# A fused two-block layer on one core: the second block's input norm and the gate bias moved to VectorE, prefix sums and clears to GpSimd, the residual's norm to the output projection, the first head pair reordered

## The reference

```python
def chunked_spatial_gating(xc, ln_g, ln_b, w_s, b_s):
    z = jax.nn.gelu(xc)
    u, v = jnp.split(z, 2, axis=-1)
    v = layernorm(v, ln_g, ln_b).reshape(B, L // CHUNK, CHUNK, N_GMLP_HEADS, GMLP_HEAD_DIM)
    g = jnp.einsum('bnpec,eqp->bnqec', v, w_s) + b_s.T[:, :, None]
    return u * g.reshape(B, L, D_GMLP)

    x = x + (jax.nn.silu(gate) * val) @ ffn_w_down[i]      # end of the first block
    return rmsnorm(x, norm_final)

def hybrid_layer(x, mem, ...):                             # the second block
    h = rms_norm(x, norm_g)
    proj = h @ w_in
    (aq, ak, av, az, br, bk, bv, bz, bwd, bad, cq, cz, ga, gb, gc) = jnp.split(proj, offsets, axis=-1)
    aq = rms_norm(aq, a_q_g); ak = rms_norm(ak, a_k_g)
    ya = chunked_band_attention(aq, ak, av, a_rel_bias) * jax.nn.silu(az)
    yb = rwkv7_time_mix(br, bk, bv, bwd, bad, ...) * jax.nn.silu(bz)
    yc = memory_cross_attention(cq, mk, mv) * jax.nn.silu(cz)
    merged = sigmoid(ga) * (ya @ w_up_a) + sigmoid(gb) * (yb @ w_up_b) + sigmoid(gc) * (yc @ w_up_c)
    return x + merged @ w_o
```

## Time and profile before

| | us |
|---|---|
| median of 3 runs (2471.11 to 2479.15) | 2474.42 |
| profiled execution | 2478.68 |
| its span, first to last instruction | 2477.0 |
| PE busy | 2413.2 |
| DVE busy | 1535.6 |
| ACT busy | 1134.2 |
| GpSimd busy | 12.8 |

### The profile page before, as it was taken

One profiled execution on the slowest core, in us unless ns is written; L12 is line 12 of the kernel. 1 busy time (PEld: TensorE's weight loads), 2 busy tenths in 40 slices (PEclk: granted clock), 3 DMA queues, 4 the chain that ended last, 5 costly groups with the idle time before them and its releaser, 6 DMA issues.

```text
span 2477.0 us, 50747 instructions
## 1 busy us (share of the span) xinstructions
PE 2413.2 (97%) x19960; PEld 2374.3 (96%) x19960; DVE 1535.6 (62%) x2064; ACT 1134.2 (46%) x1463; POOL 12.8 (1%) x27
## 2 busy tenths in 40 slices
PE   6999999999999999996999999999999999999999
PEld 6899999999999999996899999999998999999999
DVE  6556576666546666567866676766566455555554
ACT  5343345555434555434444455444465444444443
POOL 0000000000000000000000000000000000000000
PEclk9999899999999999998999999999999999999999
DMA  6453355555555555554333333332355455555554
GB/s 236 141 187 116 125 185 184 184 185 186 187 187 187 186 186 186 186 185 132 120 125 100 115 116 114 121 127 98 118 188 168 139 171 189 189 189 182 196 187 161
DMA packets 110142, 400.32 MB, mean 162 GB/s; under 512 B 12394, under 2 KB 12421, under 8 KB 109904
## 3 DMA queue, kind: packets, MB, share of 16 engines
q1 hardware_dynamic: 108000, 391.00, 47.3%
q0 software_dynamic: 2032, 7.67, 1.0%
HBM read 396.52 MB, written 2.10 MB: 161 GB/s over the span
## 4 chain that ended last, share of the span: by engine, by line
PE 92%; DVE 5%; issue 1%; ACT 1%; DMA 0%; DVEq 0%; SPq 0%; ACTq 0%
PE bank L418 91%; DVE scratch L1393 1%; DVE w_lo L1344 1%; ACT w_hi L917 1%; PE bank L620 1%; DVE h_lo L1390 0%; DVE s_k L1393 0%; DMA x<-in_xT 0%; DVE cum L1390 0%; DVE ping L1390 0%; DVE s_t L1390 0%; DVE root L1432 0%; DVE qr L1871 0%; DVE acc L1390 0%; DVE s_t L1397 0%
## 5 line engine op out<-in xcount | busy, mean ns | idle before, releaser
L1344 DVE TENSOR_TENSOR w_lo<-raw,w_hi 128x1024 fp32r<-128x1024 f32 x736 | 896.4, 1224 | 787.9 <-ACT w_hi L917 783.1
L917 ACT ACTIVATE w_hi<-raw 128x1024 fp32r<-128x1024 f32 x736 | 778.6, 1060 | 1086.0 <-PE bank L418 1062.3
L418 PE MATMUL bank<-h_hi,w_hi 128*128 128x256 f32 x4016 | 1149.8, 286 | 19.8 <-issue 8.3
L418 PE MATMUL bank<-h_lo,w_hi 128*128 128x256 f32 x4016 | 1125.9, 280 | 0.0
L418 PE MATMUL bank<-h_hi,w_lo 128*128 128x256 f32 x4016 | 1122.0, 279 | 0.0
L418 PEld LDWEIGHTS bank<-h_hi,w_hi 128*128 128x128 f32 x4016 | 758.7, 189 | 28.8 <-issue 14.2
L418 PEld LDWEIGHTS bank<-h_lo,w_hi 128*128 128x128 f32 x4016 | 759.1, 189 | 3.3 <-issue 2.2
L418 PEld LDWEIGHTS bank<-h_hi,w_lo 128*128 128x128 f32 x4016 | 758.3, 189 | 0.0
L418 PE MATMUL bank<-m_hi,w_hi 128*128 128x256 f32 x704 | 197.8, 281 | 0.0
L418 PE MATMUL bank<-m_lo,w_hi 128*128 128x256 f32 x704 | 197.1, 280 | 0.0
L418 PE MATMUL bank<-m_hi,w_lo 128*128 128x256 f32 x704 | 195.7, 278 | 0.0
(11 more groups left out here) (413 smaller groups left out, 2773.1 us busy)
## 6 DMA issues: line engine op xcount, KB each, us to landing
raw<-in_units SPq DMA_DIRECT2D x736, 512.0 KB, 3.3
x<-in_xT SPq DMA_DIRECT2D x4, 512.0 KB, 5.9
memx<-in_memT POOLq DMA_DIRECT2D x4, 512.0 KB, 7.4
out_y<-obuf SPq DMA_DIRECT2D x8, 256.0 KB, 4.2
bias_t<-in_bias POOLq DMA_DIRECT2D x8, 192.0 KB, 2.8
dft<-in_dft POOLq DMA_DIRECT2D x1, 1024.0 KB, 7.7
decay<-in_decay POOLq DMA_DIRECT2D x1, 768.0 KB, 5.8
con<-in_con SPq DMA_DIRECT2D x1, 546.0 KB, 8.1
```

The source lines that it names most:

```text
L418: return pe.matmul(out, lhsT, rhs, start=start, stop=stop, skip_group_check=True)
L917: return act.activation(out, in_, ACT.Copy, scale=scale)
L1344: dve.tensor_tensor(w_lo[slot][:, :, :], raw[slot][:, :, :], w_hi[slot][:, :, :].bitcast(F32), ALU.subtract).then_inc(split_done, 1)
```

## The change

1. The gate bias `bs` is loaded to all partitions, and DVE adds it when it reads the bank; the one-row matmuls go.
2. During the last down projection `x` times the two gains (without any norm) is split into `h_hi`/`h_lo`, quarter by quarter. `root3` is applied instead by DVE wherever a product of the second block leaves PSUM: `lx`, pr, pk, pv, k0, qk, avf, az, `cqs`, `czs`, and each merge gate. ACT no longer reads these banks; it applies Square, Tanh or Silu to what DVE wrote. `root3` moves to memory of its own, and the row root of the first block to `row_root`, over parameters no longer used.
3. The narrow projection's units 0 to 2 come first, then unit 0 of the first pair, then narrow unit 3 (SP's order of loading follows). The norm's sums on PE come after the first pair's unit 1, the rate matmuls at k = 3 to 5, three at a time.
4. Prefix sums are on GpSimd, the first pair's alone first; six clears and the ones of `ep` too. GpSimd's loads of the bias for heads 1 to 7 stand behind them in its queue.
5. In each pair the sum of the squared queries on PE goes from k = 12 to 13, its root on ACT to k = 13 behind the exponentials, the reciprocal on DVE from `late` to k = 14.
6. `x` is scaled by the first block's norm in the output projection, a pair of tiles ahead of each addition.

```diff
@@ gpsimd
+            pool.dma_start(bs[:, :, :].rearrange("p e q -> p (e q)"), a["bs"].broadcast_to([P, HY * P]))\
...
+            for t in ("a", "b", "k", "v", "Nt", "Kt"):
+                pool.memset(bd[t][:, :, :], 0.0).then_inc(zeroed, 1)
...
+            pool.wait_ge(rates_ready, 1)
+            for pairs, other in ((slice(0, 1), ping[0]), (slice(1, 8), ping[1])):
+                here, there = (t.rearrange("p g (c t) -> p (g c) t", t=CHUNK)
+                               for t in (cum[:, pairs, :], other[:, :, :]))
+                for b in range(6):
+                    src, dst = ((here, there), (there, here))[b % 2]
+                    s = 1 << b
+                    pool.tensor_tensor(dst[:, :, s:CHUNK], src[:, :, s:CHUNK], src[:, :, 0:CHUNK - s], ALU.add)\
+                        .then_inc(prefix_step, 1)
+                    pool.tensor_copy(dst[:, :, 0:s], src[:, :, 0:s]).then_inc(prefix_step, 1)
+                    steps += 2
+                    pool.wait_ge(prefix_step, steps)
+                pool.memset(spare[:, 2:3], 0.0).then_inc(prefix_done, 1)
@@ tensor
-                    mm(o, gvt[:, c, e * P:(e + 1) * P], ws[:, e, :], True, False)
-                    m = mm(o, con[0:1, CC["ones"][0]:CC["ones"][0] + P], bs[0:1, e * P:(e + 1) * P], False, True)
+                    m = mm(o, gvt[:, c, e * P:(e + 1) * P], ws[:, e, :])
...
-            norm_sums(acc_x, acc_g)
-            group(1, h_hi, h_lo, tiles=1, arriving=True)
+            def lora_unit(u):
+                pe.wait_ge(dve_for_pe, tiles_in[2 * u + 1])
+                unit(2, UK * u, h_hi, h_lo, u == 0, u == 3, 1)
+            for u in range(3):
+                lora_unit(u)
...
-                if k == 12:
+                if k == 13:
                     pe.wait_ge(sums_read, n.next("sums"))
                     pe.wait_ge(qk_squared, n.next("qk"))
...
-                from_act()
+                pe.wait_ge(bank_read[1], n.now(("fill", 1)))
                 for c in range(2):
                     m = pe.transpose(banks[7][:, c * P:(c + 1) * P], avf[:, c * P:(c + 1) * P], ident)
...
             for k in range(16):
                 heads(k)
+                if k == 0:
+                    lora_unit(3)
                 if k == 1:
+                    norm_sums(acc_x, acc_g)
+                if k == 3:
                     from_act()
                     pe.wait_ge(lora_in, 16)
@@ scalar, heads(k, g)
                 if k == 11:
-                    act.activation(qr[:, :, :], p2(0), ACT.Square).then_inc(qk_squared, 1)
-                    copy(qk[:, :, :], p2(0)).then_inc(bank_read[0], 1)
-                if k == 12:
-                    act.wait_ge(qk_sums, n.next("qk"))
-                    to_dve(act.activation(flat(qr), banks[7][:, :], ACT.Sqrt, bias=con_("eps6"), scale=1.0 / P))
+                    act.wait_ge(bank_read[0], n.now(("fill", 0)))
+                    act.activation(qr[:, :, :], qk[:, :, :], ACT.Square).then_inc(qk_squared, 1)
                 if k == 13:
+                    if isinstance(g, int):
+                        act.wait_ge(zeroed, 7)
+                    act.wait_ge(prefix_done, 1 if isinstance(g, int) else 2)
...
                     to_dve(m)
+                    act.wait_ge(qk_sums, n.next("qk"))
+                    to_dve(act.activation(flat(qr), banks[7][:, :], ACT.Sqrt, bias=con_("eps6"), scale=1.0 / P))
                 if k == 15:
-                    to_pe(copy(avf[:, :], p2(1)[:, 0, :]))
-                    to_dve(act.activation(az[:, :], p2(1)[:, 1, :], ACT.Tanh, scale=0.5))
+                    from_dve()
+                    to_dve(act.activation(small["en"][:, :], az[:, :], ACT.Tanh, scale=0.5))
@@ vector
+                    if half:
+                        for s, b in enumerate(pair):
+                            own_bank(b)
+                            gained_pair(4 * q + 2 * s, lambda t: gains[:, 1, bass.ds(t, 1)])
+                        for s in range(2):
+                            low_pair(4 * q + 2 * s)
+                        for s in range(2 if q < 3 else 0):
                             running(4 * q + 2 * s, q == 0 and s == 0, gained=True)
...
+            split4()
+            running(12, False, gained=True)
+            running(14, False, gained=True)
             to_pe(dve.memset(lx[:, 0:1], 0.0))
...
-            normalised(x, lambda t: gains[:, 1, t:t + 1], scratch2, h_hi, h_lo, root3)
-            step(dve.reciprocal(root2[:, :], root2[:, :]))
@@ vector, heads(k, g)
+                if k == 3:
+                    step(tt(sm["pr"][:, 1:T + 1], p2(0)[:, 0, :], root3[:, :], ALU.mult))
+                    read(tt(sm["pk"][:, 1:T + 1], p2(0)[:, 1, :], root3[:, :], ALU.mult), 0)
+                if k == 7:
+                    to_act(tt(sm["k0"][:, :], p2(1)[:, 1, :], root3[:, :], ALU.mult))
+                    read(tt(sm["pv"][:, 1:T + 1], p2(1)[:, 0, :], root3[:, :], ALU.mult), 1)
+                if k == 11:
+                    read(tt(qk[:, :, :], p2(0), bcast(root3[:, :], 2), ALU.mult), 0)
+                if k == 15:
+                    to_act(tt(az[:, :], p2(1)[:, 1, :], root3[:, :], ALU.mult))
+                    read(tt(avf[:, :], p2(1)[:, 0, :], root3[:, :], ALU.mult), 1)
...
+                if k == 14:
+                    from_act()
+                    step(dve.reciprocal(flat(qr), flat(qr)))
@@ vector, late(units, g)
-                read(stt(az[:, :], az[:, :], 1.0, p2(1)[:, 1, :], ALU.add, ALU.mult), 1)
-
-                step(dve.reciprocal(flat(qr), flat(qr)))
+                step(stt(az[:, :], sm["en"][:, :], 1.0, az[:, :], ALU.add, ALU.mult))
@@ vector, merge and output
+                        group_done()
+                        read(tt(gate[:, :, :], p2(0), bcast(root3[:, :], 2), ALU.mult), 0)
                         split4(2)
-                        own_bank(0)
+                        from_act()
...
+            step(dve.reciprocal(row_root, row_root))
+            settle()
+            def normed_pair(tile):
+                for s in range(2):
+                    t = x[:, bass.ds(tile + s, 1), :].rearrange("p o t -> p (o t)")
+                    step(stt(t, t, col("norm_final", tile + s), row_root, ALU.mult, ALU.mult))
+                settle()
```

More of the change, by code:

```diff
@@ L603, in _ @@
                         m.then_inc(unit_used, 1)
-            norm_sums(acc_x, acc_g)
-            group(1, h_hi, h_lo, tiles=1, arriving=True)
+            tiles_in = [n.next("dve") for _ in range(8)]
+            pe.wait_ge(bank_read[2], n.now(("fill", 2)))
+            n.next(("fill", 2))
+            def lora_unit(u):
[3 more added lines that the diff above has]
+                lora_unit(u)
             ident = con_("ident")
@@ L1272, in _ @@
                     high_halves(scratch3, mh_hi, quarters=MEM_SPLIT[h])
[L1273 removed]
                 n.next(("fill", h % 2))
[L1275 removed]
+                act.wait_ge(bank_read[h % 2], n.now(("fill", h % 2)))
+                cz = czs[:, 2 * h:2 * h + 2, :]
+                act.activation(cz, cz, ACT.Silu).then_inc(cross_gates, 1)
             def key_root():
@@ L1629, in _, with residual @@
             gated(2, last=True)
-            def residual(tile, b, out=None):
+            def residual(tile, b):
                 group_done()
@@ L1634, in residual @@
                 t = x[:, bass.ds(tile, 2), :]
-                dst = t if out is None else out[:, bass.ds(tile, 2), :]
-                read(tt(dst, t, p2(b), ALU.add), b)
+                read(tt(t, t, p2(b), ALU.add), b)
             step(dve.memset(acc_x[:, :, :], 0.0))
@@ L1839, in queries @@
                 if k % 4 == 3:
-                    n.next(("fill", (k // 4) % 2))
+                    h, b = k // 4, (k // 4) % 2
+                    n.next(("fill", b))
+                    group_done()
+                    read(tt(cqs[:, 2 * h:2 * h + 2, :], p2(b), bcast(root3[:, :], 2), ALU.mult), b)
             def y_tile(i):
@@ L2050, in _ @@
             settle_pe()
-            with n.loop(4, {"unit": 36, "act": 2, "to_act": 2, "step": 2, ("fill", 0): 6, ("fill", 1): 6,
+            with n.loop(4, {"unit": 36, "act": 8, "to_act": 2, "step": 2, ("fill", 0): 6, ("fill", 1): 6,
                             "merged": 2}) as i:
@@ L2072, in _, with output @@
                     dve.wait_ge(merged_ready, n.next("merged"))
-            with n.loop(3, {"unit": 8, ("fill", 0): 1, ("fill", 1): 1}) as i:
+            step(dve.reciprocal(row_root, row_root))
+            settle()
+            def normed_pair(tile):
+                for s in range(2):
+                    t = x[:, bass.ds(tile + s, 1), :].rearrange("p o t -> p (o t)")
+                    step(stt(t, t, col("norm_final", tile + s), row_root, ALU.mult, ALU.mult))
+                settle()
+            def output(tile, b):
+                n.next(("fill", b))
+                pair = bass.ds(tile, 2)
+                read(tt(obuf[:, pair, :], x[:, pair, :], p2(b), ALU.add), b)
```

(12 more changed lines are left out.)

176 lines of the change are left out of this document (84 added, 92 removed).

## The result

Nine runs of the changed kernel have a median of 2484.8 us (2477.67 to 2486.63), nine of the kernel before, on the same chip, 2476.86: ratio 1.0033, 95% interval 1.0019 to 1.0047. I had forecast 2466.5 with a range up to 2482. So the time lies outside the range, on the side of rival (c). As a change, the forecast was 7.9 us less, and the medians say 7.9 more.

A forecast was written before the change was run, and what follows sets the result against it. PE, busy 97% of the span, was taken to bound the kernel. Terms -14 - 26.8 + 24.5 + 4.2 + 1.2 + 0.6 - 0.6 + 3 = -7.9 us gave 2466.5 from a median of 2474.4; range 2446 to 2482.

The forecast's parts named there:

- rival (c): Between the blocks: GpSimd's sums shut DVE out, costing 17.2 us in place of 3; 2480.7 us, chance 0.13.
- Part 1: At the gate: without one-row bias matmuls PE saves 14 us, bounds 7.4 and 15, with no fall of the clock.
- Part 2: Between the blocks, down projection to head loop: 67.4 us in place of 94.2, 26.8 saved.
- Part 5: Prefix sums on GpSimd: 3 us of cost to DVE taken, between 0 and 13.1.
- Units 4 to 15 and unit 0 of head 1 follow without a wait: Between the blocks, after the rate matmuls: no PE waits, since DVE has lost 13.1 us of prefix sums.
- Part 3: Head loop: early reciprocal and products delay the masks, PE waits 3.5 us a head; seven heads cost 24.5.
- The first head's 4.2: First head: cost of 4.2 us, as ACT is later behind unit 13.
- Part 4: The rest: down projection +1.2 us, cross attention +0.6, first head's qk wait -0.6; merge gates and output hidden.
- The quarters of the down projection: Last down projection: scalings, subtractions and waits for ACT's copies cost 0.6 us for two of three quarters, 1.2.
- Cross attention: One more DVE product of 0.6 us before ACT's Silu, behind which PE waits for a split: 0.6.
- Rival (a): Head loop: the heads don't pay, or half; 2438 us, or 2452 for half, chance 0.20.

The follow-up runs named there:

- part 1 alone: The kernel before with only the gate bias changed (loaded to all partitions, added by DVE, one-row matmuls gone): median 2461.04 us, ratio 0.9939.
- e3: The changed kernel with the prefix sums left out altogether, so not computing the layer: median 2467.28 us, ratio 0.9966.
- e7: The changed kernel with reciprocal back behind the masks, prefix sums back on DVE, ACT's tanh of az moved later: median 2446.88 us, ratio 0.9878.
- e16: e7 repeated without an edit: profiled execution 2445.64 us.

## Why the prediction failed

**Part 1, right.** Predicted -14 at the gate; measured -11.7 to -12.8. PE in order of time, beside the earlier trace rows:

```profile
258.09 2.84 PE L447 MATMUL bank<-ws,gvt 128*128 128x128 f32 x24
260.77 1.89 PE L447 MATMUL bank<-pool_d,pw 128*128 128x256 f32 x8
262.31 0.47 PE L447 MATMUL bank<-h_hi,w_hi 128*128 128x256 f32 x1
```

From the gate to the next projection 4.22 us in place of 18.0, where I had 4.2, and no fall of the clock. PE comes to the gate 2.9 us later than before (258.09 against 255.21), about 1.5 of it because the clock from 60 to 90 us was 0.89 where it had been 0.94 (30 us by 0.05); the kernel with part 1 alone shows 257.83 and 0.89, the changed kernel's second profile 258.35 and 0.83. I had not looked at that stretch, and why the clock is lower there stays open.

**Part 2, right by itself, with some luck.** I predicted 67.4 us from the down projection's end, which is 65.0 from DVE's last addition (1126.46 in that trace, 2.4 behind 1124.1). Without sums it is 66.1, with the predicted waits (0.7, 3.4, 0.8, 0.5 for 0.8, 3.7, 0.7, 1.5). The 65.0 hold 1.2 for a fall of the clock at the wait for the sums; in e3 the clock did not fall, so the other terms were 2.3 too low. In the changed kernel it fell there and cost 1.5.

**Part 5, the step that failed.** "I take 3, nearer to nothing", with 13.1 as the upper bound. The gap is 21.1 us longer with the sums in the first profile and 19.7 in the second, and some 18 to 20 of that is theirs, where the sum has 3. I had the mechanism as rival (c), with 17.2 us and 2480.7, at 0.13. Two arguments misled me. The short first part (an eighth) with DVE "idle a quarter of the time" averages over a stretch; yet GpSimd's long part began right behind the short one, at 1151.6, in the unit where DVE makes the keys that PE waits for. And I took the old duration on DVE as the bound, though being shut out can cost up to what GpSimd needs (busy 24 of 24.7 us from 1151.6 to 1176.3, DVE's own instructions holding it up in turn, against 13.1 on DVE), and the clock fell behind the waits besides, some 6.5 us that I had priced at 0. "Units 4 to 15 and unit 0 of head 1 follow without a wait" failed with it, as the same three waits show.

**Part 3, right, and too high.** Period 77.9 predicted, 77.8 measured, with the waits for `avf` (1.1) and for the masks (1.7) where they were expected. The first head's 4.2 did not come (75.3 against 75.5 to 76.3): heads in all +20 in the loop and about 3 behind it, for 28.7.

**Part 4.** The quarters of the down projection cost 2.0 us (1.2 predicted); two waits of 0.51 and 0.61 stand where I had named two of 0.6, and the other 0.9 is in no wait. Cross attention has one wait for a split of 1.75 us where 0.67 stood, 1.1 for 0.6. The end of the program is as before.

**The chances.** Rival (a), heads free, had 0.20 and was far off in this kernel, though e7 shows that it needed only two lines of order. Rival (c) had 0.13; the row that spoke against it, the gaps between GpSimd's instructions, is short: 0.3 to 0.4 us between the first additions of 3.1 to 3.3, filled by their small copies.

## To carry to other kernels

Work given to GpSimd is free only if what runs on VectorE meanwhile reads at most one operand from SBUF and is no `tensor_scalar` of an SBUF tile; otherwise price it at up to GpSimd's own duration (24 us here, of which 18 to 20 showed), and put the price on the instruction that PE waits for at that moment, with the fall of the clock behind the wait. When a slow instruction is moved ahead of others on its engine, read the loop in order from there to the first thing that PE waits for; the period came out within 0.1 us that way. And before an operation is moved to another engine, look for a form of it that is short: the scan took 5.1 us where twelve instructions took 13.1.

## What the hardware showed that I had not expected

- Blocked instructions show as long ones: a 0.35 us `tensor_scalar` as 3.24, a 1.23 us split as 4.08, with no idle time beside them.
- The unit stream has two rates, 0.1167 and 0.1178 us a matmul, at granted clock 1.00; a stretch of 600 us keeps one of them, and runs of the same kernel differ by it (6.4 to 7.7 and about 4.6 us here).
- A chain of a few waits cost some 6.5 us in clock for 12.9 in waits: 504 records took 71.2 us busy at clock 0.90, 507 took 63.3 at 1.00, and 1.5 of these 8 us lie behind a wait that both kernels have.
- Behind the same wait of 3.4 us the clock fell in some runs and not in others, of one kernel too (e7 and e16), which goes with 1.4 to 1.7 us here.
